# Modulation vectors of a two-layer block: the vectors become the stationary operand, in four column groups of the array

## The chip, the cores and the metric

One core of one Trainium2 chip runs the whole kernel. The metric is the device time of one execution in microseconds (us). In the profile, PE is TensorE (PEld its weight loads), DVE VectorE, ACT ScalarE, POOL GpSimd and SP the engine that issues the DMAs.

## What is computed

Two layers act on 512 latent and 128 context tokens of width 1024. Each layer makes from a conditioning vector `c` (latent tokens) and `c_ctx` (context tokens) three vectors of 1024 numbers: shift, scale and gate.

```python
mod = (silu(c) @ w_mod[l] + b_mod[l])          # 3 * 1024 numbers, once for c, once for c_ctx
shift, scale, gate = split(mod, 3)
h = x * (1 + scale) + shift
proj = h @ w_in[l]
...
merged = sum(sigmoid(merge) * y_br, axis=2)    # three branches: Hyena convolution, two attentions
out = merged @ w_out[l]
x = layer_norm(ALPHA * x + gate * out, ln_g[l], ln_b[l])
```

All of it is float32. The change touches only how `silu(c) @ w_mod` is computed and where those steps stand.

## The kernel before

Channels lie on partitions, the 640 tokens along the free axis. A weight matrix is cut into tiles of 1024 x 128 (512 KB, `W[:, g % NW]`, three buffers, loaded by SP in the order `STREAM`). A projection (`project`, L673) computes 128 output channels: ACT rounds the tile to a high part (`high_part`, L1034), POOL subtracts it for a low part (`low_part`, L1603), and PE runs 32 matmuls with the high part (L686, L687) and 16 with the low part (L691); for a branch tile (`mbranch`, 512 x 128) it is half of each. `w_hi` and `w_lo` signal the two parts. SP may reload a buffer when `w_lo` says that POOL is done, or, for a modulation tile, when PE has used it.

Every engine walks through one hand-written list, `STEPS[l]` (L101 to L149), and does its part of each step in that order. PE's results go round four PSUM slots (`PS0` to `PS3`, `slot_table`): PE may begin a step only when the consumer of the step four slots back is done (`freed`, L521). The table `UPTO` (L260) says at which place in the list ACT and POOL make the parts of the next tile: at the place of the tile before, ahead of ACT's own work there, if at most one step lies between two tiles, and one place later, behind ACT's own work for the tile before, if more lie between (L268).

The modulation vectors come in three kinds of steps:

- `pmrow` and `pmod` (first layer, shift and scale): eight groups of 256 outputs. The vector pair `ccol` (128 x 2 per eighth of the contraction) is stationary, the weights move; PE's two rows are copied by ACT into `pmrow`, and turned by a transpose. They stand at the start, among the steps that make the convolution filters (`ffn`, `filt`).
- `gmod` (gate, both layers, eight each) and `nmod` (shift and scale of the next layer, sixteen in layer 0): the weight tile is stationary, the pair moves, eight matmuls with two columns (L768). DVE adds the bias (L1294).

In the list, latent attention (`attention_steps("ml", ...)`) is mixed with the gates and products of the second branch (`mgate`, `mbranch`) and with these steps: in layer 0 six `gmod` and ten `nmod`, in layer 1 six `gmod`. Half of them stand behind the product with the values (`ml_pv`), half behind a branch product, a transpose and the short score of the context tokens. Then comes the last part, `path` 8 to 11 and `mgate`/`mbranch` 16 to 23 (one step per tile, no other steps between), then `gmod` 6 and 7 and, in layer 0, `nmod` 10 and 11; then the output tiles `wo` 0 to 7 with their transposes `xt`. `wo` 0 needs `mg_ready`: the sum of the branches as high and low parts, made by DVE and POOL behind `mbranch` 23. At `wo` 2 of layer 0, SP waits for that too and then issues the tables of the next layer (`layer_tables`, L583), with the tile of `wo` 2 behind them. The last four `nmod` stand behind the layer norm (`ln`).

## Time and profile before

| | |
|---|---|
| time, median of 3 runs | 2186.32 us (2184.79 to 2188.69) |
| span of the profiled execution | 2188.1 us |
| PE busy | 2072.3 us, 95% of the span |
| DVE, ACT, POOL busy | 1030.0, 634.1, 517.6 us |
| chain that ended last | PE 79%, DVE 11%, ACT 3% |
| old modulation matmuls, L768 | 512 instructions, 65.4 us busy |
| first-layer rows, L777 | 256 instructions, 33.7 us busy |

The span goes from the first to the last instruction of the profiled execution; the page gives no other time of that execution. Matmul ends are modelled and overlap the next start, so the pace of PE is read from start to start. A row of a timeline gives start, length, engine, line and group, and in brackets the idle time before it with what ended it; a row of the stretches gives length, busy time and instructions of PE, PEld, DVE, ACT and POOL, then the granted clock, the DMA share and GB/s. A matmul of float32 operands stands as two instructions in the trace (16 for the eight of L768), one of the rounded parts as one.

### The profile page before, as it was taken

The page shows a single profiled execution, that of the slowest core. Times are in us where ns is not written, and L with a number is a line of the kernel's source. Part 1 is how long each engine was busy: PE and PEld are TensorE (multiplying, and loading weights), DVE is VectorE, ACT ScalarE, POOL GpSimd, SP SyncE. Part 2 cuts the span into 40 slices and gives each one's busy share as a digit, 9 for nine tenths or more (in the row PEclk, how much of TensorE's full clock was granted, in tenths as well). Part 3 has the DMA queues.
Part 4 walks back from the last instruction along what each step waited for, and adds up shares of the span by engine and source line. Part 5 has one row for each costly group of instructions (what it writes and reads, how often), then busy time and mean ns, then how long its engine had stood idle before and what let it go on. Part 6 is the DMA issues. An engine that isn't in the chain of part 4 may idle for free.

```text
span 2188.1 us, 28690 instructions
## 1 busy us (share of the span) xinstructions
PE 2072.3 (95%) x11844; PEld 1743.4 (80%) x11844; DVE 1030.0 (47%) x1486; ACT 634.1 (29%) x1075; POOL 517.6 (24%) x248
## 2 busy tenths in 40 slices
PE   6899999999999999999989999999999999999995
PEld 4578689887896778699976786898788777778995
DVE  3548587344343343321256676844443444442325
ACT  2221222334323333322133222123332233342221
POOL 0221124221231111154222111331222311013541
PEclk9999999999999999999989999999999999999997
DMA  8001012111211111232531010221112111112331
GB/s 316 30 30 39 29 49 87 53 44 38 93 59 49 56 49 68 73 106 83 168 126 39 29 39 30 68 66 51 39 49 102 44 32 39 49 44 74 129 116 48
DMA packets 45760, 149.44 MB, mean 68 GB/s; under 512 B 6590, under 2 KB 8126, under 8 KB 44480
## 3 DMA queue, kind: packets, MB, share of 16 engines
q1 hardware_dynamic: 45632, 147.62, 20.2%
q8 instruction: 94, 1.54, 0.3%
q14 instruction: 34, 0.28, 0.0%
HBM read 141.02 MB, written 6.59 MB: 67 GB/s over the span
## 4 chain that ended last, share of the span: by engine, by line
PE 79%; DVE 11%; ACT 3%; issue 2%; POOL 2%; DMA 1%; SPq 1%; DVEq 0%; ACTq 0%; POOLq 0%
PE PS L686 16%; PE PS L691 16%; PE PS L687 16%; PE PS L739 6%; PE PS L722 5%; PE PS L755 5%; PE PS L857 3%; PE PS L710 3%; PE PS L969 2%; PE PS L768 2%; PE PS L824 1%; DVE work L1650 1%; ACT work L1022 1%; PE PS L959 1%; DVE work L1648 1%
## 5 line engine op out<-in xcount | busy, mean ns | idle before, releaser
L1601 POOL TENSOR_TENSOR Wl<-W,Wh 128x1024 fp32r<-128x1024 f32 x196 | 438.4, 2239 | 1464.7 <-ACT Wh L1022 1438.6
L686 PE MATMUL PS<-Hh,Wh 128*128 128x320 f32 x2112 | 636.7, 316 | 8.8 <-ACT Wh L1022 3.8
L687 PE MATMUL PS<-Hl,Wh 128*128 128x320 f32 x2112 | 624.7, 310 | 0.0
L686 PEld LDWEIGHTS PS<-Hh,Wh 128*128 128x128 f32 x2112 | 399.3, 189 | 35.0 <-issue 21.7
L687 PEld LDWEIGHTS PS<-Hl,Wh 128*128 128x128 f32 x2112 | 399.6, 189 | 2.5 <-issue 1.2
L691 PE MATMUL PS<-Hh,Wl 128*128 128x320 f32 x2112 | 331.4, 309 | 0.9 <-POOL Wl L1601 0.9
L691 PEld LDWEIGHTS PS<-Hh,Wl 128*128 128x128 f32 x2112 | 315.1, 188 | 1.4 <-POOL Wl L1601 1.4
L1022 ACT ACTIVATE work<-PS 128x640 f32<-128x640 f32 (+9 forms) x266 | 171.5, 654 | 403.4 <-PE PS L722 99.6
L1255 DVE TENSOR_REDUCE st<-PS 128x1 f32<-128x640 f32 (+1 forms) x160 | 114.8, 718 | 197.1 <-PE PS L739 148.5
L1022 ACT ACTIVATE Wh<-W 128x1024 fp32r<-128x1024 f32 x196 | 185.8, 950 | 52.6 <-PE PS L691 27.0
L739 PE MATMUL PS<-work 64*128 64x320 f32 (+1 forms) x512 | 157.7, 440 | 4.2 <-DVE work L1553 2.3
L1121 ACT ACTIVATE th<-PS 128x640 f32<-128x640 f32 x64 | 45.0, 704 | 353.9 <-PE PS L691 353.9
L1022 ACT ACTIVATE raw<-PS 128x320 f32<-128x320 f32 (+4 forms) x98 | 38.2, 444 | 342.6 <-PE PS L691 302.9
L722 PE MATMUL PS<-work,MG 128*128 128x512 f32 x256 | 116.3, 613 | 13.0 <-ACT work L1022 6.6
L739 PEld LDWEIGHTS PS<-work 64*128 64x128 f32 (+1 forms) x512 | 90.7, 189 | 40.7 <-issue 9.2
L686 PE MATMUL PS<-BRh,Wh 128*128 128x320 f32 x384 | 119.3, 324 | 1.4 <-ACT raw L1209 1.2
L755 PE MATMUL PS<-work 128*64 128x512 f32 (+1 forms) x240 | 112.8, 618 | 2.8 <-ACT work L1022 2.8
L687 PE MATMUL PS<-BRl,Wh 128*128 128x320 f32 x384 | 114.3, 311 | 0.0
L722 PEld LDWEIGHTS PS<-work,MG 128*128 128x128 f32 x256 | 49.5, 196 | 74.1 <-issue 59.2
L710 PE MATMUL PS<-ident,work 128*128 128x128 f32 (+2 forms) x592 | 88.3, 282 | 11.9 <-DVE th L1322 8.1
L1439 DVE SCALAR_TENSOR_TENSOR th<-th,PS 128x640 f32<-128x640 f32 x32 | 26.3, 821 | 153.7 <-PE PS L691 153.7
L710 PEld LDWEIGHTS PS<-ident,work 128*128 128x128 f32 (+2 forms) x592 | 72.8, 153 | 24.8 <-DVE th L1322 9.5
(174 smaller groups left out, 2569.3 us busy)
## 6 DMA issues: line engine op xcount, KB each, us to landing
W<-in_w_in SPq DMA_DIRECT2D x132, 512.0 KB, 3.5
W<-in_w_mod SPq DMA_DIRECT2D x32, 512.0 KB, 3.6
W<-in_w_branch SPq DMA_DIRECT2D x48, 256.0 KB, 2.6
pmod_w<-in_w_mod SPq DMA_DIRECT2D x8, 1024.0 KB, 17.2
W<-in_w_out SPq DMA_DIRECT2D x16, 512.0 KB, 3.6
work<-in_x_sample SPq DMA_DIRECT2D x2, 2048.0 KB
x_mid<-work SPq DMA_DIRECT2D x1, 2560.0 KB, 9.1
work<-x_mid SPq DMA_DIRECT2D x1, 2560.0 KB
```

Of the source, the lines that this page charges most:

```text
L686: pe.matmul(out, Wh[:, b, kk, :], xh[:, kk, t], start=kk == 0, stop=False)
L687: pe.matmul(out, Wh[:, b, kk, :], xl[:, kk, t], start=False, stop=False)
L691: last = pe.matmul(out, Wl[:, b, kk, :], xh[:, kk, t], start=False, stop=kk == k - 1)
L710: return pe.transpose(out, in_, ident[0:p, 0:p])
L722: last = pe.matmul(ps[:, 512 * par:512 * par + HY], fwd[:, t, q, 128 * m:128 * m + 128], srcs[q][:, t, :], start=half == 0, stop=half == 1)
L739: last = pe.matmul(ps[:, 512 * a:512 * a + HALF], q[:, 128 * t:128 * t + 128], k[:, HALF * a:HALF * a + HALF], start=True, stop=True)
L755: pe.matmul(ps[0:m, 0:LAT], v[:, kt, c0:c0 + m], pt[:, kt, :], start=kt == 0, stop=kt == NT - 1)
L857: pe.matmul(ps[:, 256 * par:256 * par + 256], PM[:, par, q, 512 * m + 128 * c:512 * m + 128 * c + 128], inv[:, m, q, 256 * par:256 * par + ...
L1022: return act.activation(out, in_, ACT.Copy, scale=scale)
L1121: act.activation(halves(th[:, n % 2]), two(ps), ACT.Tanh, scale=0.5)\
L1255: return dve.tensor_reduce(out, two(ps) if n > CTX else ps[:, 0:n], mybir.AxisListType.XY if n > CTX else AX, ALU.max, negate=True)
L1601: return pool.tensor_tensor(out, in_, high.bitcast(f32), ALU.subtract)
```

## The change

It does four things. (1) `gmod` and `nmod` are split in two steps each. `grow`/`nrow` holds the conditioning pair stationary, padded with zeros to 32 columns (`cst`), and moves the weight tile (128 columns): eight matmuls, of which number k writes to the PSUM partitions from 32 * (k % 4), two of them to each quarter. ACT copies the 128 x 128 result into `mrow` (the memory of `lpj`). Then `gmod`/`nmod` is one matmul, `mrow` stationary and the constant `sel` (128 x 2) moving, which adds the quarters. (2) `pmrow` does the same with 256 columns, and `pmod` uses `sel` in place of the transpose. (3) The places change: in both layers all eight `grow` and eight `gmod` stand in latent attention, all `grow` behind the values (the first behind a score), all `gmod` behind the short score; the sixteen `nrow`/`nmod` pairs of layer 0 are woven into its last part; nothing stands behind `mbranch` 23 in layer 1 or behind `ln`. (4) One constant more is loaded, and one memset more runs at the start.

```diff
-    gmods = [("gmod", g) for g in range(KD)]
-    nmods = [("nmod", g) for g in range(2 * KD)] if l < DEPTH - 1 else []
-    s += head(0, 2) + head(0, NT - 1) + attention_steps("ml", MH, weave(merge_steps(1), gmods[:KD - 2] + nmods[:NMOD_EARLY - 2]), head)
-    s += path_steps(2) + merge_steps(2) + gmods[KD - 2:] + nmods[NMOD_EARLY - 2:NMOD_EARLY]
+    gmods = [step for g in range(KD) for step in (("grow", g), ("gmod", g))]
+    nmods = [step for g in range(2 * KD) for step in (("nrow", g), ("nmod", g))] if l < DEPTH - 1 else []
+    s += head(0, 2) + head(0, NT - 1) + attention_steps("ml", MH, weave(merge_steps(1), gmods), head)
+    s += weave(path_steps(2) + merge_steps(2), nmods)
     for d in range(KD):
         s += [("wo", d)]
         if d:
             s += [("xt", d - 1)]
         if l < DEPTH - 1:
             s += {3: [("nffn", 0)], 4: [("nsin", 0)], 5: [("nffn", 1)], 6: [("nsin", 1)]}.get(d, [])
-    return s + [("xt", KD - 1), ("ln", 0)] + nmods[NMOD_EARLY:]
-
-
-NMOD_EARLY = 12
...
-    if kind in ("nmod", "gmod"):
-        return [("mod", i + (2 * KD if kind == "gmod" else 0))]
+    if kind in ("nrow", "grow"):
+        return [("mod", i + (2 * KD if kind == "grow" else 0))]
...
+MODS = [(l, kind, i) for l in range(DEPTH) for kind, i in STEPS[l] if kind in ("nmod", "gmod")]
...
+    "nrow": lambda i: [("nrow_ready", i + 1)],
+    "grow": lambda i: [("grow_ready", i + 1)],
...
+    sel = (np.arange(128)[:, None] % 32 == np.arange(2)).astype(f)
...
-        ccol = sb("ccol", [128, KD, 2])
+        cst = sb("cst", [128, KD, 32])
+        sel = sb("sel", [128, 2])
...
+        mrow = lpj[:].rearrange("p a b -> p (a b)")
...
-                    if kind in ("nmod", "gmod"):
+                    if kind in ("nrow", "grow"):
                         pe.wait_ge(*freed(l, kind, i))
                         ps = slot(l, kind, i)
                         g = TILE_AT[l, kind, i]
                         pe.wait_ge(w_here[g % NW], 16 * (g // NW + 1))
                         for k in range(KD):
-                            last = pe.matmul(ps[:, 0:2], W[:, g % NW, k, :], ccol[:, k, :],
-                                             start=k == 0, stop=k == KD - 1)
+                            c = 32 * (k % 4)
+                            last = pe.matmul(ps[c:c + 32, 0:128], cst[:, k, :], W[:, g % NW, k, :],
+                                             start=k < 4, stop=k >= KD - 4)
                         last.then_inc(full_of(l, kind, i), 1)
+                    elif kind in ("nmod", "gmod"):
+                        pe.wait_ge(*freed(l, kind, i))
+                        pe.wait_ge(*after("nrow_ready" if kind == "nmod" else "grow_ready", l, i + 1))
+                        pe.matmul(slot(l, kind, i)[:, 0:2], mrow, sel[:], start=True, stop=True)\
+                          .then_inc(full_of(l, kind, i), 1)
                     elif kind == "pmrow":
                         pe.wait_ge(*freed(l, kind, i))
                         ps = slot(l, kind, i)
                         pe.wait_ge(pmod_here[i % NP], 16 * (i // NP + 1))
-                        for m in range(2):
-                            for k in range(KD):
-                                last = pe.matmul(ps[0:2, 128 * m:128 * m + 128], ccol[:, k, :],
-                                                 pmod_w[:, i % NP, m, k, :], start=k == 0, stop=k == KD - 1)
+                        for k in range(KD):
+                            c = 32 * (k % 4)
+                            last = pe.matmul(ps[c:c + 32, 0:256], cst[:, k, :], pmod_w[:, i % NP, :, k, :],
+                                             start=k < 4, stop=k >= KD - 4)
                         last.then_inc(full_of(l, kind, i), 1)
                     elif kind == "pmod":
                         pe.wait_ge(*freed(l, kind, i))
                         ps = slot(l, kind, i)
                         pe.wait_ge(*after("row_ready", 0, i + 1))
                         for m in range(2):
-                            last = transpose(ps[:, 2 * m:2 * m + 2], pmrow[:, i % 4, 128 * m:128 * m + 128], 2)
+                            last = pe.matmul(ps[:, 2 * m:2 * m + 2], pmrow[:, i % 4, 128 * m:128 * m + 128], sel[:],
+                                             start=True, stop=True)
...
-            act.activation(ccol[:], csig[:], ACT.Sigmoid).then_inc(c_sig, 1)
+            act.activation(cst[:, :, 2:4], csig[:], ACT.Sigmoid).then_inc(c_sig, 1)
...
-                        copy(pmrow[:, i % 4], slot(l, kind, i)[0:2, 0:256]).then_inc(sems["row_ready"], 1)
+                        copy(pmrow[:, i % 4], slot(l, kind, i)[:, 0:256]).then_inc(sems["row_ready"], 1)
+                    elif kind in ("nrow", "grow"):
+                        n = MODS.index((l, {"nrow": "nmod", "grow": "gmod"}[kind], i))
+                        act.wait_ge(*filled(l, kind, i))
+                        if n:
+                            act.wait_ge(*filled(*MODS[n - 1]))
+                        copy(mrow, slot(l, kind, i)[:, 0:128]).then_inc(sems["nrow_ready" if kind == "nrow" else "grow_ready"], 1)
...
-            TT(ccol[:], ccol[:], csig[:], ALU.mult).then_inc(c_silu, 1)
+            TT(cst[:, :, 0:2], cst[:, :, 2:4], csig[:], ALU.mult).then_inc(dve_chain, 1)
+            chain["dve"] += 1
+            dve.wait_ge(dve_chain, chain["dve"])
+            dve.memset(cst[:, :, 2:32], 0.0).then_inc(c_silu, 1)
```

ACT, in the last part of layer 0, where `th` is the gate's tanh, `Wh` the high part of the next tile and `lpj` the copy of a row step. Before, from the tanh of `path` 11 to that of `mgate` 17:

```order
L1121 ACTIVATE th<-PS 128x640 [waits gate_used,psum_full2]
L1022 ACTIVATE Wh<-W 128x512 [waits psum_full2,weights_here1]
L1121 ACTIVATE th<-PS 128x640 [waits gate_used,psum_full3]
L1022 ACTIVATE Wh<-W 128x1024 [waits psum_full3,weights_here2]
L1022 ACTIVATE Wh<-W 128x512 [waits psum_full0,weights_here0]
L1121 ACTIVATE th<-PS 128x640 [waits gate_used,psum_full1]
```

Now, from the tanh of `path` 11 to the tile of `mgate` 17:

```order
L1139 ACTIVATE th<-PS 128x640 [waits gate_used,psum_full2]
L1034 ACTIVATE Wh<-W 128x1024 [waits psum_full0,weights_here1]
L1034 ACTIVATE lpj<-PS 128x128 [waits psum_full1,psum_full3]
L1139 ACTIVATE th<-PS 128x640 [waits gate_used,psum_full1]
L1034 ACTIVATE Wh<-W 128x512 [waits psum_full2,weights_here0]
L1034 ACTIVATE lpj<-PS 128x128 [waits psum_full0,psum_full2]
L1034 ACTIVATE Wh<-W 128x1024 [waits psum_full1,weights_here2]
```

A `Wh` of 512 columns belongs to a branch tile. It stood ahead of the gate's tanh; now it stands behind it where a pair of new steps follows the gate, and the copy behind both.

PE at the end of the same part, with the PSUM slots: `mbranch` 23 and what leads to `wo` 0. Before:

```order
L687 MATMUL PS2<-BRl_57,Wh_53 128x320
L691 MATMUL PS2<-BRh_56,Wl_54 128x320 x8
L768 MATMUL PS3<-ccol_66,W_52 128x2 x8
L768 MATMUL PS0<-ccol_66,W_52 128x2 x8
L768 MATMUL PS1<-ccol_66,W_52 128x2 x8
L768 MATMUL PS2<-ccol_66,W_52 128x2 x8
L686 MATMUL PS3<-MGh_82,Wh_53 128x320
```

Now:

```order
L692 MATMUL PS0<-BRl_57,Wh_53 128x320
L696 MATMUL PS0<-BRh_56,Wl_54 128x320 x8
L774 MATMUL PS1<-W_52,cst_66 32x128 x8
L780 MATMUL PS2<-sel_67,lpj_75 128x2
L691 MATMUL PS3<-MGh_82,Wh_53 128x320
```

Four old steps stood there; now one pair does.

## Rows read from the trace of the kernel before

**Rows 1.** stretches: latent attention, layer 0's last part, attention of layer 1
```profile
675.60:929.40 253.80, 249.29 (x1369) 193.76 (x1367) 98.38 (x192) 90.58 (x168) 29.07 (x16) 0.97 0.18 60
...
929.40:1042.20 112.80, 112.80 (x771) 112.79 (x770) 23.54 (x33) 24.61 (x32) 53.82 (x30) 1.00 0.29 94
...
1746.80:1980.40 233.60, 228.81 (x1210) 173.54 (x1208) 95.99 (x182) 89.12 (x168) 29.49 (x16) 0.99 0.13 43
```

**Rows 2.** timeline of PE: one old modulation step in layer 0's attention
```profile
696.31 1.84 PE L768 MATMUL PS<-ccol,W 128*128 128x2 f32 x16
...
698.01 0.74 PE L710 MATMUL PS<-ident,work 128*128 128x128 f32 x5
```

**Rows 3.** timeline of PE: one group of first-layer rows
```profile
29.38 3.65 PE L777 MATMUL PS<-pmod_w,ccol 128*2 128x128 f32 x32
```

**Rows 4.** timeline of PE: sums in 32 columns; broadcasts from four row groups
```profile
483.34 1.26 PE L698 MATMUL PS<-work,ones 128*32 128x320 f32 x4
...
484.17 0.43 PE L698 MATMUL PS<-work,ones 128*32 128x320 f32 x1
...
484.53 0.41 PE L686 MATMUL PS<-BRh,Wh 128*128 128x320 f32 x1
...
598.69 1.98 PE L705 MATMUL PS<-raw,ones 1*128 1x320 f32 x16 [0.15 <-DVE raw L1502]
```

**Rows 5.** timeline of PE and DVE behind mbranch 10, layer 0
```profile
765.12 0.71 PE L710 MATMUL PS<-ident,raw 128*128 128x128 f32 x5
...
766.24 1.60 DVE L1440 TENSOR_TENSOR MG<-MG,th 128x640 f32<-128x640 f32 x1
...
767.99 0.74 PE L710 MATMUL PS<-ident,work 128*128 128x128 f32 x5 [0.25 <-DVE MG L1440]
```

**Rows 6.** timeline of PE behind mbranch 14, layer 1
```profile
1888.97 0.81 PE L739 MATMUL PS<-work 96*128 96x320 f32 x2 [1.20 <-DVE MG L1440]
```

**Rows 7.** timeline of ACT, last part; its 128x128 copies by form
```profile
1028.27 0.70 ACT L1121 ACTIVATE th<-PS 128x640 f32<-128x640 f32 x1 [6.35 <-PE PS L691]
...
1028.87 1.05 ACT L1022 ACTIVATE Wh<-W 128x1024 fp32r<-128x1024 f32 x1
...
1031.85 0.63 ACT L1022 ACTIVATE Wh<-W 128x512 fp32r<-128x512 f32 x1 [1.93 <-PE PS L691]
...
L1022 ACT ACTIVATE work<-PS 128x128 f32<-128x128 f32 x24 | 6.5, 269 | 1.1 <-PE PS L710 1.1
```

**Rows 8.** timeline of PE, POOL, SP, ACT from mbranch 23, layer 0
```profile
1042.15 9.95 PE L768 MATMUL PS<-ccol,W 128*128 128x2 f32 x64
...
1044.70 1.54 POOL L1601 TENSOR_TENSOR MGl<-MG,MGh 128x640 fp32r<-128x640 f32 x1 [7.72 <-DVE MGh L1443]
...
1049.14 0.38 SPq L591 DMA_DIRECT2D vecs<-in_vecs  x1
...
1055.50 1.39 SPq L559 DMA_DIRECT2D W<-in_w_out  x3
...
1068.82 1.06 ACT L1022 ACTIVATE Wh<-W 128x1024 fp32r<-128x1024 f32 x1 [6.41 <-DMA W<-in_w_out]
```

**Rows 9.** timeline of PE at wo 0, layer 1
```profile
2093.10 3.63 PE L768 MATMUL PS<-ccol,W 128*128 128x2 f32 x32
...
2098.26 0.64 PE L686 MATMUL PS<-MGh,Wh 128*128 128x320 f32 x1 [1.54 <-POOL MGl L1601]
```

**Rows 10.** timeline of PE and DVE between the layers
```profile
1124.45 10.30 PE L768 MATMUL PS<-ccol,W 128*128 128x2 f32 x64
...
1129.95 4.21 DVE L1587 TENSOR_SCALAR work<-work,lnmv,lnr 128x1024 f32<-128x1024 f32 x5
```

**Rows 11.** timeline of PE and ACT at the first filters
```profile
42.70 5.30 PE L777 MATMUL PS<-pmod_w,ccol 128*2 128x128 f32 x32 [3.05 <-DMA pmod_w<-in_w_mod]
...
48.32 1.13 ACT L1083 ACTIVATE work<-BR,negt 128x1024 f32<-128x1024 f32 x1
...
68.29 1.22 PE L722 MATMUL PS<-work,MG 128*128 128x512 f32 x1 [4.61 <-DVE work L1364]
```

19 lines of the change are left out of this document (10 added, 9 removed).

## The prediction

> **What bounds the kernel.** I read the stretches first. In layer 0's last part PE is busy 112.80 of 112.80 us, in latent attention 249.29 of 253.80 and 228.81 of 233.60 [rows 1]. So PE's own order sets the time almost everywhere, and whatever stands in it is paid in full, unless PE would have waited there anyway. The second look therefore goes to the few places with a wait behind the old steps: which wait ends there next? Layer 1 tests this: its latent attention has ten old steps fewer and is 20.2 us shorter, 2.0 us a step [rows 1].
>
> **Unit prices.** An old step is 16 instructions; from its start at 696.31 to the next group's at 698.01 are 1.70 us, and 1.8 behind a product with the values, which changes the tile shape: 1.75 on average [rows 2].
> The row step also has 16 instructions, each moving 128 float32 columns. Such an instruction takes 0.11 us: 32 of them fill 3.65 us with the last one's 0.27 [rows 3]. One after the other that is 1.74 us, and nothing is saved. The gain hangs on four column groups running at once. No row shows that for columns, but one shows it for groups of partitions: four broadcasts in four row groups, 16 instructions of 320 columns, started within 1.98 - 0.43 = 1.55 us, 0.10 each, though one of that size takes (1.26 - 0.43) / 3 = 0.28 within one group [rows 4]. I take columns to behave likewise: four instructions deep in each group, 0.44 us, and 0.1 for issuing. Changing to 32-column tiles and back costs about 0.09 each: behind the last of the sums the next start comes after 0.36 instead of 0.27 [rows 4]. With that and rounding up, 0.8 us. The bounds are 0.6 and 1.9 (serial, with the changes).
> The new `gmod`/`nmod` is two instructions that load 128 columns, 2 x 0.11 = 0.22 us [rows 2]. A pair costs 1.02 us of PE where one step cost 1.75; and ACT copies 128 x 128 in 0.27 between the two [rows 7].
>
> The Trainium skill ("TensorE: Matmul & The Clock Gate", Part 3) says that matmuls start and end in strict program order. The row of the broadcasts speaks against it: four instructions of one group, each 0.27 behind the last, cannot all start ahead of the next group's in 1.55 us for sixteen. By the rule a row step would be about 0.35 us dearer; that is a rival below. The same section gives 2.38 times for three column tiles at once; no run here shows it, and by it the sum would stay as it is.
>
> **Latent attention, layer 0.** Sixteen old steps become eight row steps and eight sums, in the same places. Behind the values nothing waits: 8 x (1.8 - 0.8) = 8.0 us saved. Behind a branch product it is different. There PE runs a transpose and the short score (0.77 us) and then the modulation step; the next transpose needs the PSUM slot that DVE frees by adding the product to `MG`. Behind `mbranch` 10 that product ended at 765.12; DVE's addition ended at 767.84 (1.60 us long), and the transpose came at 767.99 [rows 5]. So the old step filled a wait of 2.9 us, and with 0.22 in its place the transpose still comes at 2.9. The gain is nil at three such places and at the last, 0.4 at the first, and 1.5 at each of the three where a key projection (2.6 us) lies between: 4.9. The clock stood at 0.97 here against 0.99 in layer 1 [rows 1]; part of the difference may go with the dense runs of two-column matmuls, and I add 1.6. Sum: -14.5 us; bounds -9 and -19, and +0 to -5 if the row step is serial.
>
> **Latent attention, layer 1.** Six old steps (one of them hidden at the end) leave: -8.7. Eight row steps and seven sums come: 8 x 0.8 + 7 x 0.22 = +7.9. The wait behind the branch product exists there already without an old step (1.20 us idle until DVE's `MG`, [rows 6]), at two places; after the change at four, 1.3 to 1.9 us each, 7.0 instead of 2.7: +4.3. Sum +3.5; bounds 0 and +6.
>
> **Last part of layer 0.** Here everything is added. Fifteen pairs lie inside, 15 x 1.02 = 15.3 us. To this come waits that were not there. ACT now makes the high part of the next tile behind the gate's tanh wherever two new steps follow a gate: 0.2 after the gate's end tanh 0.70, then the high part 0.63 (1.05 for a full tile), then the copy 0.27 [rows 7], then the sum on PE. Where row step and sum stand together behind a gate (`path` 11, `mgate` 16, 18, 21, 23) the next product starts 2.25 to 2.7 us after it instead of 1.0: 4 x 1.3 + 1.7 = 6.9. Where sum and the next row step stand there (`path` 9, `mgate` 17, 22) no copy is waited for: 2.5. Where a pair stands behind `mbranch` 18 and 20 PE waits for the copy alone, 0.6 each: 1.3. POOL takes the low part of the next tile behind the `MG` part (1.54, [rows 8]) where it stood ahead of it, and a tile's DMA waits for a row step three tiles back: 1.3 for all. Sum 15.3 + 12.0 = +27.3; bounds +20 (0.6 a row step, waits half as long) and +34.
>
> **Behind it.** In layer 0 four old steps took 1042.15 to 1051.96. Without them `wo` 0 could start when the `MG` part is done, at 1046.24. But `wo` 2 ends that gain: its tile lands behind the tables, which SP issued at 1049.14; the high part began at 1068.82, 19.7 us later [rows 8]. Tables issued at once at 1046.3 give a `wo` 2 at 25.2 us behind `mbranch` 23 where it was 27.8. Gain 2.6 and not 5.7. In layer 1 two old steps stood where PE waited for `MG` until 2098.26 in any case [rows 9]: nothing is gained. Between the layers the four old steps ended at 1134.6, and the layer norm at 1134.16 [rows 10]: 0.7 with DVE's four additions of the bias.
>
> **Start.** Groups of rows took 3.65 us (5.30 after an idle time) and now about 1.1. The first waits for its DMA until 42.70 as before. From there each filter waits for the decay of ACT (1.13) and four operations of DVE (2.8), a cycle of 4.2 us where PE's was 5.7, so that the first transform comes 5 us ahead of 68.29 [rows 11]. Less 0.4 for one DMA more at the head, and something for a slower clock with PE idle: -4; bounds 0 and -6.
>
> **The sum.** -14.5 + 3.5 + 27.3 - 2.6 - 0.7 - 4.0 = +9.0 us. It is made against the profiled span of 2188.1, 1.8 above the median of the runs; I put it on the median: 2186.3 + 9.0 = **2195.3 us**. The arithmetic saved, 0.73 us times 32 steps, is 23 us; the places give it back.
>
> **Rivals.**
> - *Matmuls start in program order.* The second instruction of a group holds up the next group, so that eight matmuls follow each other at 0.11: with the last one's 0.11 and the two changes of tile 1.15 a row step. Eight and eight in attention, some seven uncovered in the last part: 23 x 0.35 = 8, and 3 at the start: 2206. For it: the engine has one queue. Against it: the broadcasts. 0.17.
> - *Column groups are no concurrency at all.* That the change doesn't do what it says: a row step costs 1.9. 23 x 1.1 = 25, the start's 4, and 2 where the waits don't cover: 2226. For it: no row shows columns side by side. 0.11.
> - *Not slower: the clock.* The old steps are two-column matmuls. If they are what lowers the clock to 0.97 in layer 0's attention (253.8 x 0.03 x 2 = 15 us at half clock, over 7 us lost), 6 us come back instead of 1.6, and DVE's addition, no longer hit at its worst, takes 0.82 instead of 1.60 behind six products, 4 us more. That gives 2187, no change; with a row step of 0.6 it gives 2182. It decides if more than 5 of its 8 us come. 0.15.
> - *The forecast*, 2188 to 2203: 0.57.
>
> **Range and chances.** I leave out the serial case and half of the fastest: 2183 to 2213. A measurement of this kernel tells 0.2%, 4.4 us, from no change. Slower: three quarters of the forecast's share and the two dear cases, 0.70. Same: the forecast's low end and most of the clock case, 0.21. Faster: 0.09.
>
> **What would show it.** Row steps: 16 starts within some 0.5 us, or 0.9 (program order), or 1.7 (serial). The last part of layer 0: 140 us instead of 112.8, with PE idle for the high part (ACT) and the copy behind gates. Latent attention: both layers near 238 us, idle on DVE's `MG` behind four products in each. `wo` 2 still waits for its tile, by the DMA. First transform near 64. I am wrong if the last part grows by less than 18 us, or if attention in layer 0 stays above 245.

## The result, and the profile after

The changed kernel takes 2210.26 us (median of 4, 2209.0 to 2212.21), the kernel before on the same chip 2187.51 us (2184.79 to 2190.56): ratio 1.0105, 95% interval 1.0091 to 1.012. It is 22.8 us slower, where 9.0 was forecast. The profiled execution spans 2208.1 us against 2188.1, so the traces show 20.0 of them. Below, an old step is the `gmod` or `nmod` of the kernel before, a row step is `grow` or `nrow`, and a sum is the new `gmod` or `nmod`. Cut at the same places of the program, to about 0.1 us, the stretches are as follows.

| stretch | before | after | change | forecast |
|---|---|---|---|---|
| start to latent attention, layer 0 | 675.6 | 676.4 | +0.8 | -4.0 |
| latent attention, layer 0 | 253.9 | 241.6 | -12.3 | -14.5 |
| last part, layer 0 | 112.6 | 139.5 | +26.9 | +27.3 |
| from there to latent attention, layer 1 | 704.6 | 701.3 | -3.3 | -3.3 |
| latent attention, layer 1 | 233.7 | 243.1 | +9.4 | +3.5 |
| last part, layer 1 | 112.6 | 112.6 | 0 | 0 |
| behind it | 95.0 | 93.6 | -1.4 | 0 |

Two terms missed most, the start by 4.8 and layer 1's attention by 5.9 us; layer 0's attention missed by 2.2. The stretches of after that answer to [rows 1] (columns as there: length, busy time of PE, PEld, DVE, ACT, POOL, granted clock, DMA share, GB/s):

```profile
676.40:917.90 241.50, 225.56 (x1258) 169.34 (x1256) 96.59 (x184) 91.59 (x176) 29.03 (x16) 0.99 0.14 46
917.90:1057.40 139.50, 128.67 (x1038) 121.79 (x1038) 28.80 (x48) 28.40 (x48) 53.60 (x30) 1.00 0.42 132
1758.70:2001.80 243.10, 226.85 (x1258) 168.93 (x1256) 96.58 (x184) 91.59 (x176) 29.05 (x16) 0.98 0.14 46
```

PE was busy 112.80 of 112.80 us in layer 0's last part; now it is busy 128.67 of 139.50. Both attentions run the same list of steps now and wait the same: 241.50 - 225.56 = 15.9 us and 16.3, where 4.5 and 4.8 stood before.

PE in one row step, layer 0's attention:

```profile
697.18 0.64 PE L774 MATMUL PS<-W,cst 128*32 128x128 f32 x16
697.75 0.33 PE L715 MATMUL PS<-ident,work 128*128 128x128 f32 x1
```

From its start to the start of the next group are 0.57 us, less than the lower bound of the forecast (0.6). So the arithmetic saved more than was forecast, and still the kernel is slower.

PE's waits in the changed last part of layer 0, and in layer 1's attention after and before (us in total, times, longest):

```profile
PE PS L780 <- ACT lpj L1034: 7.3, 7, 1.4
PE PS L691 <- ACT Wh L1034: 2.6, 4, 1.1
PE PS L696 <- POOL Wl L1622: 0.8, 2, 0.4
```

```profile
PE PS L715 <- DVE MG L1461: 7.9, 5, 1.7
PE PS L744 <- ACT work L1034: 3.4, 3, 1.1
PE PS L691 <- ACT raw L1227: 2.5, 1, 2.5
```

```profile
PE PS L739 <- DVE MG L1440: 1.9, 2, 1.2
PE PS L739 <- DVE work L1553: 1.1, 1, 1.1
```

In the last part the sum (L780) waits for ACT's copy. At `path` 11 it looks like this, ACT first, then PE:

```profile
949.97 0.70 ACT L1139 ACTIVATE th<-PS 128x640 f32<-128x640 f32 x1 [6.55 <-PE PS L696]
950.57 1.05 ACT L1034 ACTIVATE Wh<-W 128x1024 fp32r<-128x1024 f32 x1
951.51 0.27 ACT L1034 ACTIVATE lpj<-PS 128x128 f32<-128x128 f32 x1
```

```profile
949.86 0.64 PE L774 MATMUL PS<-W,cst 128*32 128x128 f32 x16
951.93 0.35 PE L780 MATMUL PS<-sel,lpj 128*128 128x2 f32 x2 [1.42 <-ACT lpj L1034]
```

The row step's last matmul started at 950.2, but ACT first makes the tanh and the whole high part; the next product starts 2.3 us behind the row step. That is the sequence of the order listings, with the prices of [rows 7].

At the start nothing was gained. PE before, behind the sixth group of rows:

```profile
48.14 1.99 PE L824 MATMUL PS<-BR 64*128 64x512 f32 x4
50.06 3.66 PE L777 MATMUL PS<-pmod_w,ccol 128*2 128x128 f32 x32
```

And now, from the sixth group of rows to the first transform, which answers to [rows 11]:

```profile
44.77 1.93 PE L788 MATMUL PS<-pmod_w,cst 128*32 128x256 f32 x16 [1.53 <-DMA pmod_w<-in_w_mod]
46.64 1.01 PE L796 MATMUL PS<-sel,work 128*128 128x2 f32 x4
47.58 3.77 PE L836 MATMUL PS<-BR 64*128 64x512 f32 x4
51.29 1.93 PE L788 MATMUL PS<-pmod_w,cst 128*32 128x256 f32 x16
...
71.81 8.56 PE L727 MATMUL PS<-work,MG 128*128 128x512 f32 x16 [2.77 <-DVE work L1385]
```

The group of rows is short (1.87 us to the next), but the filter's product, which the change doesn't touch, takes 3.77 us; it took 1.99. A cycle is 51.29 - 44.77 = 6.5 us where it was 5.7. The trace has no record of the clock ahead of 74.7 us (the column of the granted clock prints 1.00 for such a stretch), so here durations are the evidence: PE ran at about half speed from the start into the first transform. The +0.8 us of this stretch is not exact: six of the kernels below have the same start stage, and in their traces latent attention begins between 674.0 and 677.7 us (676.4 here).

### The profile page after: what moved, and what is told of

Its sections match the earlier page's. It is cut to its first block, busy times and chain, and to the rows that moved or that the text cites. A ratio compares the mean times of both kernels' runs of the same rounds, so it can differ in the third digit from the quotient of the medians.

```text
span 2208.1 us, 28700 instructions
## 1 busy us (share of the span) xinstructions
PE 2037.4 (92%) x11796; PEld 1691.7 (77%) x11796; DVE 1033.1 (47%) x1487; ACT 640.6 (29%) x1107; POOL 516.7 (23%) x248
## 4 chain that ended last, share of the span: by engine, by line
PE 76%; DVE 11%; issue 4%; ACT 3%; POOL 2%; SPq 1%; DMA 1%; DVEq 0%; ACTq 0%; POOLq 0%
PE PS L691 16%; PE PS L696 15%; PE PS L692 15%; PE PS L744 6%; PE PS L727 5%; PE PS L760 5%; PE PS L869 3%; PE PS L715 3%; PE PS L981 2%; PE PS L836 2%; ACT work L1034 1%; POOL Wl L1622 1%; DVE work L1671 1%; ACT Wh L1034 1%; PE PS L971 1%
## 5 line engine op out<-in xcount | busy, mean ns | idle before, releaser
L1034 ACT ACTIVATE work<-PS 128x640 f32<-128x640 f32 (+8 forms) x266 | 171.7, 654 | 386.7 <-PE PS L727 99.1
L715 PE MATMUL PS<-ident,work 128*128 128x128 f32 x576 | 86.1, 284 | 31.0 <-DVE MG L1461 10.3
L715 PEld LDWEIGHTS PS<-ident,work 128*128 128x128 f32 x576 | 69.7, 152 | 43.7 <-issue 28.3
L691 PE MATMUL PS<-MGh,Wh 128*128 128x320 f32 x256 | 79.9, 325 | 14.7 <-POOL MGl L1622 7.5
```

The source lines that it names most:

```text
L691: pe.matmul(out, Wh[:, b, kk, :], xh[:, kk, t], start=kk == 0, stop=False)
L715: return pe.transpose(out, in_, ident[0:p, 0:p])
L1034: return act.activation(out, in_, ACT.Copy, scale=scale)
```

## The experiments

All kernels are edits of the changed one; "against after" compares medians with 2210.3 us. Each set ran beside the kernel before (medians of 2187.7 to 2190.6 us). A line `...` in a diff stands for lines of the edit that are left out.

### The start undone (x1_old_start)

```diff
-                        for k in range(KD):
-                            c = 32 * (k % 4)
-                            last = pe.matmul(ps[c:c + 32, 0:256], cst[:, k, :], pmod_w[:, i % NP, :, k, :],
-                                             start=k < 4, stop=k >= KD - 4)
+                        for m in range(2):
+                            for k in range(KD):
+                                last = pe.matmul(ps[0:2, 128 * m:128 * m + 128], cst[:, k, 0:2],
+                                                 pmod_w[:, i % NP, m, k, :], start=k == 0, stop=k == KD - 1)
...
```

> The changed kernel with the start stage undone: the first layer's rows and their turning as before (two-column stationary operand, 32 matmuls of 128 columns a group, transposes), everything else as after. Theory (clock): the new rows leave PE so little to do that its clock stays at the lower level until 75 us; with the old rows back it rises by 12 to 15 us, the products of the filter net take 1.99 us instead of 3.78, and the first transform starts near 69 to 70 us (68.3 before, 71.8 after). Rival (DMA): the delay comes from the constant loaded more, which let the sixth group of rows land at 44.6 us instead of 42.6; then the first transform stays 2 us behind the kernel before, at 70.3 or later, whatever the clock. At the end of the kernel the gain should be no more than the 0.75 us by which the latent attention starts later in the changed kernel: time 2209 to 2210 us, against 2210.3.

Measured: 2211.26 us, ratio to before 1.0103 (1.0088 to 1.0118), the same as after. PE's timeline:

```profile
44.17 3.65 PE L788 MATMUL PS<-pmod_w,cst 128*2 128x128 f32 x32 [1.38 <-DMA pmod_w<-in_w_mod]
...
47.97 1.99 PE L835 MATMUL PS<-BR 64*128 64x512 f32 x4
49.88 3.65 PE L788 MATMUL PS<-pmod_w,cst 128*2 128x128 f32 x32
...
68.11 4.64 PE L727 MATMUL PS<-work,MG 128*128 128x512 f32 x5 [4.61 <-DVE work L1384]
```

With the long groups of rows back the product takes 1.99 again and the transform comes at 68.11. The DMA is late here too (the group waits until 44.17 where it waited until 42.70 before), but the sixth group then takes 3.65 us instead of 5.30, so the late landing decided nothing. Attention begins at 675.6, and the whole time can't be told from after's: the new start stage neither gained nor lost anything that these runs can show.

### PE kept at work at the start (x2_warm_start)

```diff
...
+                    if l == 0 and WARM.get((kind, i)):
+                        pe.wait_ge(*freed(l, kind, i))
+                        for _ in range(WARM[kind, i]):
+                            pe.matmul(slot(l, kind, i)[:, 0:128], ones[:], ones[:], start=True, stop=True)
```

> The changed kernel with matmuls added whose results are overwritten: 128 by 128 constants, 10, 8, 26, 10 and 14 of them ahead of the first, second, third, fifth and sixth group of rows and 10 ahead of the first transform, where PE waits for a DMA or for DVE. Theory (clock): PE's clock rises to its upper level before the third group, a product of the filter net takes 1.99 us, the cycle of a filter falls from 6.5 us to the 4.2 of ACT and DVE, and the first transform starts at 62 to 65 us, the -4 of the forecast and more; time 2200 to 2206. Rival: the clock is not the cause, the cycle stays near 6.5 us, the transform starts at 72 or, by the added work, later; time 2210 to 2213.

Measured: 2198.84 us (2196.19 to 2205.41), ratio 1.0055 (1.0035 to 1.0075): 11.4 us less than after. PE's timeline:

```profile
50.72 1.07 PE L793 MATMUL PS<-pmod_w,cst 128*32 128x256 f32 x16
51.72 0.61 PE L801 MATMUL PS<-sel,work 128*128 128x2 f32 x4
52.26 1.99 PE L841 MATMUL PS<-BR 64*128 64x512 f32 x4
54.18 0.61 PE L801 MATMUL PS<-sel,work 128*128 128x2 f32 x4
...
62.23 7.03 PE L727 MATMUL PS<-work,MG 128*128 128x512 f32 x16
```

The same group of rows takes 1.00 us instead of 1.86, the product 1.99, and PE's cycle 3.5 us (DVE's is 4.0 now, near the 4.2 of the forecast); the transform starts at 62.23, 9.6 us ahead of after, and with its own 7.03 instead of 8.56 and a few more gains behind it latent attention begins at 663.6 instead of 676.4. Work was added and time was saved: the clock was the cause. At the upper clock the forecast's -4 would have been right in its sign, and too small.

### Sum ahead of the next row step, high part ahead of the tanh (x3_apart)

```diff
-    s += weave(path_steps(2) + merge_steps(2), nmods)
...
+        groups = [nmods[:1]] + [nmods[n:n + 2] for n in range(1, len(nmods) - 1, 2)] + [nmods[-1:]]
+        s += [x for step in weave(path_steps(2) + merge_steps(2), groups) for x in (step if type(step) is list else [step])]
...
-            table[l, a if b - a <= 2 else a + 1] = n + 2
+            table[l, a if b - a <= 2 or (b - a == 3 and STEPS[l][a + 1][0] in ("nrow", "nmod")) else a + 1] = n + 2
```

> The changed kernel, with the last part of layer 0 in another order: behind each projection first the sum of the row step before, then the next row step, and the high part of the next tile made ahead of the gate's tanh. The same steps, 15 row steps and 15 sums inside. Theory: of the 26.8 us by which this part grew, 11.5 are the steps themselves (0.57 and 0.14 to 0.21), the rest waits for ACT's copy and high part, and 2 us changes of the tile shape. With the waits gone the part takes 112.6 + 11.5 + 2.5 = 126 to 128 us instead of 139.5, time 2197 to 2200. Rival: the waits only move, since ACT's copy waits for the sum before and the slots come round faster; the part stays above 134, time above 2205.

Measured: 2204.43 us (2197.01 to 2210.22), ratio 1.0069 (1.0043 to 1.0095). The last part takes 131.1 us, 8.4 less than after, between the two expectations. The time is 5.8 us less than after's and above the expected 2197 to 2200. PE's only wait there, and ACT at one of the places:

```profile
PE PS L695 <- ACT Wh L1038: 4.0, 5, 1.8
```

```profile
958.56 1.06 ACT L1038 ACTIVATE Wh<-W 128x1024 fp32r<-128x1024 f32 x1 [3.84 <-DMA W<-in_w_in]
```

No sum waits any more. In their place the high part waits for its tile's DMA: the three buffers hold modulation tiles too, and a tile's load is issued only when the row step three tiles back has run (this one at 954.43, behind the row step of 953.73, and it landed at 958.53). That is a wait which neither theory had; 131.1 - 4.0 = 127.1 is the number of the first. The gain isn't kept in full: in this trace the stretch behind `mbranch` 23 takes 706.5 us instead of 701.3 though it has a row step less, with 48 us at the lower clock instead of 34.

### The place of the high part alone (x4_high_ahead)

```diff
-            table[l, a if b - a <= 2 else a + 1] = n + 2
+            table[l, a if b - a <= 2 or (b - a == 3 and STEPS[l][a + 1][0] in ("nrow", "nmod")) else a + 1] = n + 2
```

> The changed kernel, in the last part of layer 0 only the place of the high (and low) part changed: ahead of the gate's tanh although two new steps follow; the order of row steps and sums as it was. It tells the price of the high part's place from that of the copy. If both are as they look in the trace (2.6 us waits for the high part, 7.3 for the copy, and the copies stand 1 us behind where a high part stands ahead of them), the part falls from 139.5 to 135 to 137 and the time to 2206 to 2208. If the high part is the cause of the copies' waits too, it falls to 130 to 132, time 2201 to 2203. If nothing hangs on it, it stays at 2210.

Measured: 2208.19 us (2206.47 to 2211.4), ratio 1.009 (1.0075 to 1.0105). The last part falls from 139.5 to 131.7 us, which is the second expectation:

```profile
PE PS L780 <- ACT lpj L1034: 3.9, 7, 0.9
PE PS L691 <- ACT Wh L1034: 0.4, 1, 0.4
```

The copies' wait halves from 7.3 to 3.9, the high part's falls from 2.6 to 0.4, the low part's goes. So one line of the table of places costs 7.8 of the 26.9 us in this part. Of that 2 us arrive in the median, which the intervals don't tell from after (the time is where the first expectation had it, the last part where the second had it); the stretch behind took 704.1 us instead of 701.3 in this trace, with 44 us at the lower clock instead of 34, and the first attention 242.8 instead of 241.6.

### The order of the column groups (x5_pairs)

```diff
-                            c = 32 * (k % 4)
+                            c = 32 * (k // 2)
...
-                                             start=k < 4, stop=k >= KD - 4)
+                                             start=k % 2 == 0, stop=k % 2 == 1)
```

> The changed kernel, in the row steps of the gate and of the next layer's vectors only the order of the column groups changed: matmul k writes to group k // 2 (0, 0, 1, 1, 2, 2, 3, 3) instead of k % 4. The same work, the same sums but for their order. Each float32 matmul is two instructions, so now four instructions in a row belong to one group. Theory 1: a group's matmul starts when its own group is free, whatever stands ahead of it in the program: the 16 starts still lie within 0.37 to 0.45 us, 0.57 us to the next step, time 2210. Theory 2: PE looks only a short way ahead (two instructions of a group held up do not hold up the next, four do): the starts spread over 0.9 to 1.3 us and a row step costs 1.1 to 1.5, with some 24 of the 32 steps uncovered 12 to 22 us more. Theory 3: strict program order would already show in the changed kernel (0.11 between k and k + 1; it shows 0.007) and is excluded.

Measured, in one execution: 2215.93 us; its last part takes 139.1 us. The row step:

```profile
696.80 0.67 PE L774 MATMUL PS<-W,cst 128*32 128x128 f32 x16
697.40 0.33 PE L715 MATMUL PS<-ident,work 128*128 128x128 f32 x1
```

0.60 us against 0.57. Theory 1 holds: four instructions in a row of one group hold nothing up. The 16 starts come in four rounds of four, as in after; within a round they lie 13 ns apart instead of 7, and the rounds follow at 0.11 to 0.13 us in both. The 5.7 us more in this one execution stand in other stretches (layer 1's attention 246.7, at the lower clock for 17 us of it; its waits are those of after), and one execution doesn't settle them.

### One column group (x12_one_group)

```diff
-                            c = 32 * (k % 4)
-                            last = pe.matmul(ps[c:c + 32, 0:128], cst[:, k, :], W[:, g % NW, k, :],
-                                             start=k < 4, stop=k >= KD - 4)
+                            last = pe.matmul(ps[0:32, 0:128], cst[:, k, :], W[:, g % NW, k, :],
+                                             start=k == 0, stop=k == KD - 1)
...
-                        pe.matmul(slot(l, kind, i)[:, 0:2], mrow, sel[:], start=True, stop=True)\
+                        pe.matmul(slot(l, kind, i)[:, 0:2], mrow[0:32], sel[0:32], start=True, stop=True)\
...
```

> The changed kernel, with the row steps of the gate and of the next layer's vectors in one column group: the eight matmuls of a row step all write to partitions 0 to 31, and the sum takes these 32 alone. Steps, places, waits and the start stage stay. It prices the four groups side by side, the part of the change that the places can't give or take. Theory: the 16 instructions follow each other at 0.11 us, 1.65 from the first start to the last instead of 0.37, so a row step costs 1.85 instead of 0.57. Behind the values and in the last part that is paid in full, 8 in each attention and 15 in the last part: +10 in each attention (241.6 to 252, 243.1 to 253), +19 in the last part (139.5 to 158), time 2247 to 2251. Rival: in the last part PE waits for ACT's high part and copy in any case, so that a longer row step costs less there than it is longer: +12 to +15, time 2241 to 2245.

Measured: 2242.83 us (2237.59 to 2243.98), ratio 1.0245 (1.0228 to 1.0262), 32.6 us above after. A row step, and the two stretches of layer 0:

```profile
756.09 1.94 PE L773 MATMUL PS<-W,cst 128*32 128x128 f32 x16
757.95 0.33 PE L715 MATMUL PS<-ident,work 128*128 128x128 f32 x1
```

```profile
674.00:924.30 250.30, 237.40 (x1258) 178.52 (x1257) 96.59 (x184) 92.02 (x177) 29.04 (x16) 0.99 0.13 44
924.30:1076.90 152.60, 149.38 (x1038) 141.88 (x1038) 29.88 (x48) 29.20 (x48) 53.56 (x30) 1.00 0.36 121
```

1.86 us a row step, so the four groups side by side save 1.3 us each. The last part grows by 13.1 and not by 15 x 1.3 = 19.5: the rival is right, PE waited there for ACT anyway, and a longer row step partly fills that wait. Layer 0's attention grows by 8.8, near the 10 expected. Layer 1's grows only from 243.1 to 247.7: the granted clock doesn't fall in it, where after had 10.2 us at the lower clock.

### Row steps and sums swapped in attention (x6_swap)

```diff
-    s += head(0, 2) + head(0, NT - 1) + attention_steps("ml", MH, weave(merge_steps(1), gmods), head)
+    moved = weave(merge_steps(1), [None] + gmods[:-1])
+    s += head(0, 2) + head(0, NT - 1) + [x for x in attention_steps("ml", MH, moved, head) if x] + gmods[-1:]
```

> The changed kernel, in latent attention of both layers row steps and sums changed places: the row step behind the branch product and the short score (where PE waits for DVE's sum into MG, or for ACT's copies of the key), the sum behind the values. Theory: a step in such a wait costs nothing, so that now 0.57 us instead of 0.14 is hidden at each of eight places; each layer's attention becomes 3 to 3.5 us shorter (241.6 to 238, 243.1 to 240), time 2203 to 2205. Rival: the wait is not one of the slot behind the step, and the row step adds to it: attention stays within 1 us, time 2210, or DVE's sum gets later because a tile is read in its stead, and it grows.

Measured: 2195.57 us (2193.77 to 2197.97), ratio 1.0039 (1.0025 to 1.0054): 14.7 us less than after for a move by one place. Both attentions:

```profile
676.70:910.70 234.00, 223.09 (x1256) 166.77 (x1255) 97.53 (x183) 90.69 (x177) 29.42 (x16) 1.00 0.14 47
1751.70:1986.10 234.40, 223.13 (x1256) 166.79 (x1254) 97.53 (x183) 90.56 (x176) 29.42 (x16) 1.00 0.14 47
```

They become 7.5 and 8.7 us shorter where 3 to 3.5 were expected, and the time is below the expected 2203 to 2205. The rows split it. PE's idle time falls from 15.9 and 16.3 to 10.9 and 11.3, 5.0 in each. Its two largest waits in layer 0 are now:

```profile
PE PS L716 <- DVE MG L1462: 5.8, 5, 1.2
PE PS L745 <- ACT work L1035: 1.7, 3, 0.6
```

2.1 less for `MG` and 1.7 less for the key, about the 3.4 (8 x 0.43) that was expected; and the wait for the first exponentials, 2.2 us, is gone, with 0.9 of small ones new. The other 2.5 and 3.7 us are busy time: the same steps take less, with a granted clock of 1.00 throughout where it was 0.99 and 0.98.

### The waits filled (x9_filled)

```diff
...
+                    if WARM.get((l, kind, i)):
+                        pe.wait_ge(*freed(l, kind, i))
+                        for _ in range(WARM[l, kind, i]):
+                            pe.matmul(slot(l, kind, i)[:, 0:128], ones[:], ones[:], start=True, stop=True)
```

> The changed kernel, with 4 or 7 overwritten matmuls of constants (0.22 us each) ahead of each sum in latent attention, so that PE works where it would wait for DVE's sum into MG or for the key's copies; nothing else is changed. It tells what the waits cost beside their own length. Theory: the stretches at the lower clock in attention (6.8 us in layer 0, 10.2 in layer 1, none in the run with row steps and sums swapped) follow from these waits; with them filled 3 to 5 us come back in each layer, 241.6 to about 238 and 243.1 to about 238, time 2201 to 2204. Rival: the swapped order won its 7.6 and 8.7 us by shorter waits alone, the clock falls wherever it falls; then both attentions stay within 1 us or grow by up to 2, time 2209 to 2214.

Measured: 2209.01 us (2202.04 to 2209.33), ratio 1.0089 (1.007 to 1.0108), not told apart from after by the time. The attentions:

```profile
677.30:917.20 239.90, 233.77 (x1346) 178.07 (x1345) 96.61 (x184) 91.62 (x177) 29.06 (x16) 0.99 0.14 46
1759.40:1999.70 240.30, 233.83 (x1346) 178.07 (x1344) 96.60 (x184) 91.61 (x176) 29.08 (x16) 0.99 0.14 46
```

They are 1.6 and 2.8 us shorter, with 44 more matmuls in each. That is about half of what the theory said, in one trace: each still has 3.4 us at the lower clock, where after had 6.8 and 10.2 and the swapped kernel none. The time at the lower clock that went, 3.4 and 6.8 us, is worth 1.7 and 3.4 at half speed, about what was gained. So the waits did cost some clock beside their own length. The swapped kernel's 2.5 and 3.7 us are no more than its 6.8 and 10.2 us less at the lower clock would give (3.4 and 5.1); why its clock never fell, though it still waits, stays open.

### Row steps only where PE didn't wait (x7_mixed, x8_mixed_warm, x10_mixed_old_end)

`ROWED` names the steps that are split in two; all others stay old steps at the places of before, most of them inside the waits. The start stage is the old one again, too.

```diff
+ROWED = {(0, "gmod", 0), (0, "gmod", 2), (0, "gmod", 4), (0, "nmod", 0), (0, "nmod", 2), (0, "nmod", 4), (0, "nmod", 6),
+         (0, "nmod", 8), (0, "nmod", 10), (0, "nmod", 11), (1, "gmod", 0), (1, "gmod", 1), (1, "gmod", 3), (1, "gmod", 4)}
...
+        s += [("nrow", 10), ("gmod", 6), ("nmod", 10), ("nrow", 11), ("gmod", 7), ("nmod", 11)]
```

> The kernel before (start stage, places and old steps), with row steps and sums only where PE did not wait: in layer 0's latent attention eight of the sixteen old steps (those behind the values), two of the four behind mbranch 23, in layer 1's attention four of the six; a sum stands ahead of the next row step. The others stay old steps, inside the waits for DVE and for MG. Theory: 1.75 - 0.57 - 0.14 to 0.21 = 1.0 saved at each of 12 places in attention, 8 us in layer 0 and 4 in layer 1, and 2 to 2.5 behind mbranch 23: 2172 to 2176 us, 0.993 to 0.995 of the kernel before. Rival: the sum put ahead of a row step takes a slot of the ring of four and turns the wait for the short score's neighbour into one ahead of the next transposes; then attention gains less than 4 us in layer 0 and the time is 2180 to 2186.

Measured: 2188.8 us (2183.94 to 2190.8, 11 runs), ratio 1.0002 (0.9994 to 1.0011). No gain, where 12 to 15 us were expected. Layer 0's attention keeps most of it (247.2 for 253.9), layer 1's takes 232.5 for 233.7, and the stretch behind `mbranch` 23 grows from 704.6 to 711.5. Why, ACT and PE at its begin, and PE's first waits in layer 1's attention:

```profile
1042.10 1.06 ACT L1070 ACTIVATE Wh<-W 128x1024 fp32r<-128x1024 f32 x1 [9.03 <-DMA W<-in_w_out]
1043.06 0.26 ACT L1070 ACTIVATE lpj<-PS 128x128 f32<-128x128 f32 x1
```

```profile
1043.46 0.56 PE L817 MATMUL PS<-sel,lpj 128*128 128x2 f32 x2 [5.17 <-ACT lpj L1070]
```

```profile
PE PS L801 <- ACT work L1263: 2.3, 2, 1.2
```

The row step behind `mbranch` 23 started at 1035.8 and the next step at 1036.3. Its copy stands on ACT behind the high part of an output tile, and that high part waits for the tile's DMA until 1042.1. `wo` 0 starts 3.2 us later behind `mbranch` 23 than before; the rest of the 6.9 us lies further behind, with 51 us at the lower clock in the stretch instead of 34. And in layer 1 the sum ahead of the row step takes a slot of the ring, so that the row step waits for an exponential (2.3 us in all): the rival's mechanism, but in layer 1 and not in layer 0.

The next one has the start of the changed kernel and the added matmuls of x2_warm_start besides.

> The mixed kernel (row steps only where PE did not wait), with the start stage of the changed kernel and the overwritten matmuls that keep PE's clock up, as in the run with the warm start. Theory: the two gains add, 12 us at the start and 14 elsewhere: 2160 to 2164 us, 0.987 to 0.990 of the kernel before. Rival: part of the 12 us came back only because the changed kernel had lost it (3.5 us at the first transform); against the start of the kernel before the gain is 8 to 9, 2164 to 2168.

Measured: 2179.54 us (2177.07 to 2187.91, 12 runs), ratio 0.9968 (0.9957 to 0.9978), 9.3 below the mixed kernel. The warm start's part came as in the rival, the other part could not, since the mixed kernel has no 14 us to add.

And this one, with that start too, has the old end again:

```diff
-        s += [("nrow", 10), ("gmod", 6), ("nmod", 10), ("nrow", 11), ("gmod", 7), ("nmod", 11)]
+        s += gmods[KD - 2:] + nmods[NMOD_EARLY - 2:NMOD_EARLY]
```

> The mixed kernel with the warm start, and behind mbranch 23 the four old steps of the kernel before again (the two pairs there gone). Theory: the 6.9 us by which the stretch from mbranch 23 to layer 1's latent attention grew in the mixed kernel come from the copy of the row step, which stands on ACT behind the high part of the next output tile, and that waits for its DMA (5.2 us of PE waiting for the copy), and from the lower clock behind it; with the old steps back the stretch is 704 to 705 us again, time 2172 to 2175. Rival: the stretch stays above 709, since the start or the clock and not the copy made it longer; time 2178 to 2180.

Measured: 2173.18 us (2169.87 to 2183.88, 6 runs), ratio 0.9936 (0.9916 to 0.9956); the stretch behind `mbranch` 23 takes 705.2 us, as expected, for 709.4 in x8_mixed_warm and 711.5 in x7_mixed. `wo` 0 starts 9.9 us behind `mbranch` 23 again, where it was 13.0 in both: 3.1 us are what the copy behind a waiting high part cost. The other 1 to 3 us were not told apart from the clock. The profiled execution shows how uncertain the warm start is:

```profile
0.00:46.00 46.00, 34.28 (x266) 26.06 (x267) 15.31 (x36) 12.82 (x17) 0.20 (x4) 0.96 0.93 336
46.00:71.00 25.00, 25.00 (x82) 12.60 (x81) 11.61 (x22) 4.58 (x6) 0.00 (x0) 0.52 0.23 73
```

From 46.2 us on PE had half its clock though it was busy without a gap, and the transform came at 70.3 instead of the 60.5 of x8_mixed_warm. Four of the runs lie at 2170 to 2174 us and two, this one among them, at 2182 to 2184.

### What the runs pointed to, together (x11_combined)

Warm start; row steps behind the branch products in both attentions; eight pairs instead of sixteen in the last part, sum first and high part ahead; four old steps behind `mbranch` 23, four behind the layer norm.

```diff
...
+        pairs = [step for g in range(NROWS) for step in (("nrow", g), ("nmod", g))]
+        groups = [pairs[:1]] + [pairs[n:n + 2] for n in range(1, len(pairs) - 1, 2)] + [pairs[-1:]]
+        last = [x for step in weave(last[:-1], groups) for x in (step if type(step) is list else [step])] + last[-1:]
+        last += [("nmod", g) for g in range(NROWS, NROWS + 4)]
...
+NROWS = 8
```

> What the runs so far point to, together: the warm start; in latent attention of both layers the eight row steps behind the branch products and the sums behind the values; in the last part of layer 0 only eight pairs instead of sixteen, the sum ahead of the next row step and the high part ahead of the gate's tanh; four old steps behind mbranch 23 and four behind the layer norm, as before. Theory, stretch by stretch: start to latent attention 663.6 (675.6 before), attention 234.0 (253.9), last part 112.6 + 7 to 10 (112.6), the stretch behind it 704, attention of layer 1 234.4 (233.7), last parts 112.6 and 94: sum 2163 to 2167, time 2165 to 2169, 0.990 to 0.992 of the kernel before. Rival: tiles in the last part wait for their DMA as in the run with sums and row steps apart (4.0 us there) and the clock falls in the attentions after all: 2172 to 2176.

Measured: 2173.39 us (2168.83 to 2181.43, 6 runs), ratio 0.9938 (0.992 to 0.9957): 15.5 us faster than the kernel before, 36.9 than the changed one.

```profile
667.20:901.20 234.00, 223.08 (x1256) 166.74 (x1254) 97.50 (x183) 90.56 (x176) 29.41 (x16) 1.00 0.14 47
901.20:1021.30 120.10, 120.10 (x916) 118.21 (x916) 26.56 (x42) 26.87 (x40) 53.79 (x30) 1.00 0.37 123
1728.70:1962.70 234.00, 223.07 (x1256) 166.76 (x1254) 97.51 (x183) 90.58 (x176) 29.42 (x16) 1.00 0.14 47
```

The attentions and the last part (PE busy throughout) came as laid out. The rest of the forecast 2165 to 2169 was lost at the start (667.2 for 663.6) and behind `mbranch` 23 (707.4 for 704), where the lower clock stood for 48 us, against 34 in the kernel before. It is no faster than the mixed kernel with the old end; much of the gain of both is the warm start, which the kernel before could have too, and that wasn't run.

## Why the prediction was right or wrong

**The direction and its reason** were right: the arithmetic is saved, and the places give it back. The size was not: +22.8 us for +9.0, inside the range of 2183 to 2213 but near its upper end. The form with one column group shows the saving (32.6 us), the swapped and the reordered kernel show the places (14.7 us, some 6 of them by the clock, and 5.8 us). The mixed kernel is 21.5 us below after, but it differs in more than places, since most of its steps are old ones.

**Unit prices.** The row step was put at 0.8 and is 0.57, the sum at 0.22 and is 0.14 to 0.21; a pair costs 0.75 and not 1.02. The four groups run side by side, as [rows 4] let one expect of groups of partitions, and the instructions of a group follow at 0.11, so that 16 need 0.37 us from the first start to the last. The serial price, 1.9 in the forecast, is 1.86. The 0.57 holds what a change of tile costs at the step itself; the projections around it in the last part became dearer too (below).

**Program order** fails as a rival. The Trainium skill ("TensorE: Matmul & The Clock Gate", Part 3) says that matmuls start in strict program order. The trace names no column group, but with `k // 2` four consecutive instructions belong to one group, one group alone passes one per 0.11 us (1.86 us a row step), and yet four start within 0.04 us. They can't be those four, so here the matmuls start out of program order, against what the page says.

**Latent attention, layer 0**: -12.3 for -14.5. Busy time fell by 23.7 us, a little more than the 20.6 of steps and 1.6 of clock; the waits grew by 11.4, where the forecast holds 8 x (1.8 - 0.22) - 4.9 = 7.7. The step that failed is "1.5 at each of the three where a key projection (2.6 us) lies between": there PE now waits 1.1 each for ACT's copies of the key, which the old step had covered. The wait for the first exponentials grew by 1.0 as well (2.2 for 1.2).

**Latent attention, layer 1**: +9.4 for +3.5. Busy time fell by 2.0, the waits grew by 11.5, and 4.3 were counted. The five waits for DVE's `MG` (7.9 us) are nearly the 7.0 forecast. What was not looked for are the three for the key (3.4) and one for the first exponentials (2.5): the forecast took the places from layer 1 before, but the new list has another order there. As more steps are mixed in, the branch products stand at other places: between a key projection and the first score that needs it now stand only a short score, a sum and a transpose, where before a branch product stood at two of the three and an old step at the third. To read it, the new list should have been gone through with the ring of slots, step by step, as it was done for layer 0.

**Last part, layer 0**: +26.9 for +27.3, but by errors that cancel, which is luck. Counted from start to start, without their waits, the 15 pairs cost 12.3 us instead of 15.3. The waits are 10.8 instead of 12.0. And 3.8 us lie in the twenty projections, 116.6 us instead of 112.7 without their waits, a term that the forecast put at nothing: a whole one takes 6.99 us from its first start to its last where it took 6.89, and the step behind comes up to 0.1 later; why isn't shown. The mechanism was the one forecast, high part behind the tanh and copy behind both; it costs 7.8 by itself (x4_high_ahead). "2.25 to 2.7 us" from a row step behind a gate to the next product holds for `path` 11 alone (2.3); at `mgate` 16, 18, 21 and 23 it is 1.85 to 1.86. At `mbranch` 18 the wait for the copy is 1.4 where 0.6 was forecast.

**Behind it**: -3.3 for -3.3, and this too is partly luck. `wo` 2 starts 23.6 us behind `mbranch` 23, where 25.2 were forecast and 27.8 stood before: 4.2 gained and not 2.6. From there to layer 1's attention 0.8 are lost, where 0.7 were to be gained. The -1.4 for 0 behind layer 1's last part is no gain of the change: x1_old_start has the same steps there and takes 1.4 us longer than after.

**Start**: +0.8 for -4.0. The failing step is the cycle of 4.2 us with "something for a slower clock": the clock was taken for a correction, and it nearly doubled the durations of PE (3.77 for 1.99). [Rows 11] held the hint, a group of rows that takes 5.30 instead of 3.65 behind an idle time. PE's long groups of rows were what raised the clock: with them back the product takes 1.99 again (x1_old_start).

**The rival of the clock** was half right. It said that the old steps lower the clock in attention. In the trace of after the granted clock in layer 0's attention is 0.99 for 0.97, with 6.8 us at the lower level instead of 13.7, and busy time fell by 1.4 us more than the steps explain (23.7 against 8 x (1.8 - 0.57) + 8 x (1.7 - 0.14) = 22.3). But the clock follows the waits as well, which went the other way in layer 1 (0.98 for 0.99). The waits for `MG` stayed, up to 1.7 us each.

**What would make me wrong**: the last part grew by 26.9, more than 18, and layer 0's attention fell under 245; so neither sign of being wrong came. The start, which had no such line, is where a gain was forecast and none came.

## To carry to other kernels

A step that stands inside a wait costs nothing, so a cheaper step is worth something only at the places where nothing is waited for: put the long one into the wait and the short one outside (14.7 us for that here, some 6 of them by the clock), and count each new hand-over between engines with all that stands ahead of it in the other engine's queue. An engine whose clock follows its work can lose by having little to do all that it saves (the start stage here); compare an untouched instruction's duration in both traces (1.99 and 3.77 us) before believing a stage's sum.

## What was not expected of the hardware

- Column groups of 32 are not entered in program order: 16 float32 instructions of 128 columns in four groups start within 0.37 us (0.39 with four in a row to one group), against 1.66 in one group; within a round of four the starts lie 7 ns apart with the matmuls in the order 0, 1, 2, 3 and 13 ns in the order 0, 0, 1, 1. It looks as if each instruction in the queue cost 3.3 ns, held up or not; that is only argued.
- PE that was busy 45.80 of the first 70 us, in short pieces, stayed at its lower clock until 74.7 us; with 78 matmuls added, whose results nobody reads, it was at the upper one from 10.8 us to the first transform at 62.2, but for 13.7 us, and the whole kernel gained 11.4 us.
- Once (x10_mixed_old_end) the clock fell at 46.2 us and stayed down for 23.9 us although PE was busy throughout (25.00 of 25.00 us). No run tells why.
